# Both directions of a gated linear recurrence in one product per level, worked head by head

## What is computed

```python
def hgrn2_bidir(q, v, k_f, k_b, lf_f, lf_b, s0_f, s0_b):
    o_f = gla_chunk_scan(q, k_f, v, lf_f, s0_f)
    o_b = flip(gla_chunk_scan(flip(q), flip(k_b), flip(v), flip(lf_b), s0_b))
    return o_f + o_b
```

## Time and profile before

| what | us |
|---|---|
| median of three runs | 2602.84 |
| the profiled execution | 2599.3 |
| its span on the core | 2597.6 |
| PE busy in the span | 2484.4 |
| DVE busy | 1622.0 |
| ACT busy | 886.6 |
| the stage of the recurrence | 1287.3 to 1764.3 |

### The profile page before, as it was taken

The page is one execution under the profiler, slowest core; times in us unless marked ns, Lnnn a source line. Parts: engine busy times, 40 slices in busy tenths (PEclk is TensorE's granted clock), DMA queues, the critical chain, the costliest instruction groups (busy, mean ns, idle before and its releaser), DMA issues. The chain is left out here.

```text
span 2597.6 us, 39539 instructions
## 1 busy us (share of the span) xinstructions
PE 2484.4 (96%) x16809; PEld 1336.3 (51%) x16809; DVE 1622.0 (62%) x2112; ACT 886.6 (34%) x1061; POOL 26.8 (1%) x60
## 2 busy tenths in 40 slices
PE   7999889999999999999999999979989999999997
PEld 4457664444444444444767776764434444444443
DVE  6688747544444443645477878786766777774243
ACT  5118316332233232323354544452332222222121
POOL 0010000010000000000000000000000000000000
PEclk9999999999999999999999999999999999999999
DMA  9127563111111124343210000021101211113442
GB/s 328 31 73 235 192 212 131 33 49 49 48 48 48 48 77 111 106 120 130 56 31 18 25 26 25 18 97 50 33 17 52 61 49 48 48 55 106 112 112 87
DMA packets 302918, 207.37 MB, mean 80 GB/s; under 512 B 11296, under 2 KB 298174, under 8 KB 302143
## 3 DMA queue, kind: packets, MB, share of 16 engines
q1 hardware_dynamic: 301910, 205.08, 26.3%
q10 hardware_dynamic: 873, 0.32, 0.1%
HBM read 191.22 MB, written 13.64 MB: 79 GB/s over the span
## 5 line engine op out<-in xcount | busy, mean ns | idle before, releaser
L200 PE MATMUL ps<-hT,arena 128*128 128x512 bf16 (+1 forms) x6240 | 1337.3, 376 | 13.3 <-DVE hT L705 4.9
L200 PEld LDWEIGHTS ps<-hT,arena 128*128 128x128 bf16 x6240 | 609.1, 98 | 739.0 <-issue 17.1
L1917 PE MATMUL ps<-arena 128*128 128x512 bf16 x2112 | 458.7, 379 | 3.0 <-DVE arena L1899 3.0
L1917 PEld LDWEIGHTS ps<-arena 128*128 128x128 bf16 x2112 | 206.3, 98 | 252.2 <-DVE arena L1899 5.3
L2170 DVE SCALAR_TENSOR_TENSOR arena<-ps,vec,arena 128x945 f32<-128x945 f32 (+2 forms) x176 | 215.1, 1222 | 70.1 <-ACT arena L2156 50.7
L2137 DVE SCALAR_TENSOR_TENSOR arena<-ps,vec,arena 128x1023 f32<-128x1023 f32 (+1 forms) x88 | 106.8, 1276 | 177.8 <-ACT arena L2127 177.8
L1899 DVE TENSOR_TENSOR arena<-hT,arena 128x2816 bf16<-128x2816 f32 (+2 forms) x44 | 93.7, 2157 | 164.8 <-ACT arena L1893 164.6
L1893 ACT ACTIVATE arena<-hT 128x2816 bf16<-128x2816 f32 (+2 forms) x44 | 77.8, 1798 | 240.1 <-DMA hT<-w_down_dram 112.6
L2988 PE MATMUL ps<-arena 128*128 128x128 f32 (+1 forms) x896 | 103.2, 272 | 21.6 <-DVE arena L3309 21.6
L2084 DVE TENSOR_TENSOR arena<-hT,arena 128x2048 bf16<-128x2048 f32 x44 | 100.9, 2292 | 28.1 <-ACT arena L2051 27.8
L2988 PEld LDWEIGHTS ps<-arena 128*128 128x128 f32 (+1 forms) x896 | 98.5, 187 | 25.6 <-DVE arena L3309 24.0
(11 more groups left out here) (421 smaller groups left out, 2468.9 us busy)
## 6 DMA issues: line engine op xcount, KB each, us to landing
xT<-ada_w_dram SPq DMA_DIRECT2D x24, 1024.0 KB, 5.9
hT<-w_up_dram SPq DMA_DIRECT2D x44, 512.0 KB, 5.0
hT<-ffn_up_dram SPq DMA_DIRECT2D x44, 512.0 KB, 5.0
hT<-w_down_dram SPq DMA_DIRECT2D x30, 704.0 KB, 7.1
hT<-ffn_down_dram SPq DMA_DIRECT2D x30, 704.0 KB, 6.9
arena<-w_in_dram SPq DMA_DIRECT2D x33, 512.0 KB, 3.9
xT<-w_mod_dram SPq DMA_DIRECT2D x16, 1024.0 KB, 6.1
arena<-w_mod_dram SPq DMA_DIRECT2D x8, 1024.0 KB, 19.2
```

Of the source, the lines that this page charges most:

```text
L200: last = pe.matmul(out, lhs(a, kt), rhs(b, kt, i), start=start and kt == 0 and (a, b) == (0, 0), stop=stop and kt == n_k - 1 and (a, b) == ...
L1917: last = pe.matmul(self.bank(u), self.part(u, a, kt), self.g[:, b, kt, cols], start=kt == 0 and (a, b) == (0, 0), stop=kt == FT - 1 and (a ...
```

## The change

The two directions of a head are worked together. At a level, the keys of the forward direction stand in the left halves and its queries in the right ones, and for the backward direction the other way round. So one tile (`keys_side`) takes both directions' keys, 1024 columns full, and another (`queries_side`) both directions' queries; one product of 8 full chunks gives the scores of both, and one masked copy of 1024 columns, with the masks of both directions in one, takes them over. The diagonal adds both directions in PSUM. The scores are multiplied by the values once per head. There are 28 levels in all in place of 56, each with two exponentials.

The tiles for this need room: keys and b of both directions are kept for two heads, those of even heads in the space of the residual stream, which is away in this stage; the state's first block and the chunk decays move into the freed half of the masks; `x` has four buffers, two per level, so `subtract` of a level waits for the product two levels before. The order of a head is written anew on all engines: the projections of the next head come as V0, V1, z forward, z backward, query, gate, and those of head 0 all stand ahead of its levels. The weight tiles are loaded in this order, and the extra gates' pieces are cut anew (8 in place of 9).

```diff
-                    quarter = k.masks[:, d, l, :].rearrange("p (b h r) -> p b h r", h=2, r=m)[:, :, 1 - d, :]
+                    quarter = k.masks[:, 0, l, :].rearrange("p (b h r) -> p b h r", h=2, r=m)[:, :, 1 - d, :]
...
-    keys, b = take(2, TT), take(2, TT)
-    x = take(3, T)
+    odd_keys, odd_b = take(2, TT), take(2, TT)
+    x = take(4, T)
...
-    state0 = take(P)
-    chunk_decay = take(NCH)
+    state0 = k.masks[:, 1, 0, :]
+    chunk_decay = k.masks[:, 1, 1, 0:NCH]
+    even_keys = [scratch_x(k)(d * TT, TT) for d in range(2)]
+    even_b = [scratch_x(k)(11 * T // 2 + d * TT, TT) for d in range(2)]
...
+            def diagonal(h):
+                pe.wait_ge(k_ready, unit(h, 1) + 1)
+                pe.wait_ge(q_scaled, h + 1)
+                def both(out, c):
+                    for d in range(2):
+                        last = pe.matmul(out, x_tokens(keys(h, d))[:, c * P:(c + 1) * P], q[:, h % 2, c * P:(c + 1) * P],
+                                         start=d == 0, stop=d == 1)
+                    return last
+                chunk_job((h, "diagonal"), range(T // P), both)
+            def level(h, l):
+                pe.wait_ge(x_ready, NL * h + l + 1)
+                still, moving = keys_side(h, l), queries_side(h, l)
+                chunk_job((h, "level", l), range(T // P), lambda out, c: pe.matmul(
+                    out, still[:, c * P:(c + 1) * P], moving[:, c * P:(c + 1) * P], start=True, stop=True))
...
+            for h in range(HG_HEADS):
+                turned_keys(h, 0)
+                if h:
+                    sum_of_squares(h - 1)
+                diagonal(h)
+                level(h, 0)
+                state_products(h, 0)
+                front(h + 1, V0)
+                front(h + 1, V1)
+                level(h, 1)
+                turned_keys(h, 1)
+                carried(h, 0)
+                fill(("mid", h))
+                level(h, 2)
+                state_products(h, 1)
+                front(h + 1, ZF0)
+                front(h + 1, ZF1)
+                level(h, 3)
+                carried(h, 1)
+                front(h + 1, ZB0)
+                front(h + 1, ZB1)
+                level(h, 4)
+                front(h + 1, QUERY)
+                level(h, 5)
+                level(h, 6)
+                fill(("end", h))
+                front(h + 1, GATE)
...
+                for i, side in enumerate((keys_side(h, l), queries_side(h, l))):
+                    act.wait_ge(sub_done, 2 * (NL * h + l) + i + 1)
+                    act.activation(side, side, ACT.Exp).then_inc(exp_done, 1)
...
+            for h in range(HG_HEADS):
+                if h:
                     squares(h - 1)
+                level(h, 0)
+                turned_keys(h, 0)
+                if h:
+                    inverse_root(h - 1)
+                level(h, 1)
+                decays(h, 1)
+                front(h + 1, V0)
+                front(h + 1, V1)
+                weights_hi(h + 1, V1)
+                turned_keys(h, 1)
+                level(h, 2)
+                query_decays(h, 1)
+                level(h, 3)
...
-                front(n + 1, Z0)
-                front(n + 1, Z1)
-                softplus_parts(n + 1)
-                weights_hi(n + 1, Z1)
-                level(n, 5)
-                level(n, 6)
-                front(n + 1, V0)
-                forget_parts(n + 1)
-                front(n + 1, GATE)
...
+                front(h + 1, ZF0)
+                front(h + 1, ZF1)
+                softplus_parts(h + 1, 0)
+                weights_hi(h + 1, ZF1)
+                level(h, 4)
+                forget_parts(h + 1, 0)
+                front(h + 1, ZB0)
+                front(h + 1, ZB1)
+                softplus_parts(h + 1, 1)
+                weights_hi(h + 1, ZB1)
+                level(h, 5)
+                front(h + 1, QUERY)
+                weights_hi(h + 1, QUERY)
+                forget_parts(h + 1, 1)
+                level(h, 6)
+                decays(h + 1, 0)
+                query_decays(h + 1, 0)
+                front(h + 1, GATE)
+                weights_hi(h + 1, GATE)
...
-                i = NL * n + l - 3
+                i = NL * h + l - 2
...
+                dve.tensor_tensor(left, mid_f, left_f, ALU.subtract)
+                dve.tensor_tensor(right, mid_b, right_b, ALU.subtract).then_inc(sub_done, 1)
+                left, right = halves_of(queries_side(h, l), m)
+                dve.tensor_tensor(left, left_b, mid_b, ALU.subtract)
+                dve.tensor_tensor(right, right_f, mid_f, ALU.subtract).then_inc(sub_done, 1)
...
+                dve.wait_ge(exp_done, 2 * (NL * h + l) + 1)
+                for d in range(2):
+                    side = halves_of(keys_side(h, l), LEVELS[l])[d]
+                    dve.tensor_tensor(side, side, halves_of(x_tokens(keys(h, d)), LEVELS[l])[d], ALU.mult)
+                dve.wait_ge(exp_done, 2 * (NL * h + l) + 2)
+                side = queries_side(h, l)
+                dve.tensor_tensor(side, side, q[:, h % 2, :], ALU.mult).then_inc(x_ready, 1)
...
+            def select(h, l):
+                job = (h, "level", l)
+                by_chunk = lambda v: v.rearrange("p (c r) -> p c r", r=P)
+                mask = mask_u[:, l, :].unsqueeze(1).to_broadcast((P, T // P, P))
                 wait_made(dve, job)
-                s_, use = slot((n, "level", NL if l == 0 else l - 1))
-                dve.wait_ge(read[s_], use + 1)
-                dve.copy_predicated(queries(att), mask, queries(banks(job))).then_inc(read[slot(job)[0]], 1)
+                wait_read(dve, (h, "level", l - 1) if l else (h, "diagonal"))
+                dve.copy_predicated(by_chunk(att), mask, by_chunk(banks(job))).then_inc(read[slot(job)[0]], 1)
...
+                chain_states(h, 0)
+                weigh(h, 1)
+                decayed_keys(h, 1)
+                decayed_queries(h, 0)
+                weights_lo(h + 1, V1)
+                subtract(h, 2)
+                if h:
                     finish(h - 1)
...
-                subtract(n, 5)
-                select(n, 3)
-                subtract(n, 6)
-                softplus(n + 1)
-                weights_lo(n + 1, Z1)
-                weigh(n, 5)
-                weigh(n, 6)
-                select(n, 4)
-                forget(n + 1)
...
+                select(h, 1)
+                weigh(h, 2)
+                subtract(h, 3)
+                take_fill(("mid", h))
+                select(h, 2)
+                weigh(h, 3)
+                chain_states(h, 1)
+                decayed_queries(h, 1)
+                subtract(h, 4)
+                select(h, 3)
+                weights_lo(h + 1, ZF1)
+                softplus(h + 1, 0)
+                weigh(h, 4)
+                subtract(h, 5)
+                forget(h + 1, 0)
+                select(h, 4)
+                weigh(h, 5)
+                subtract(h, 6)
+                softplus(h + 1, 1)
+                weights_lo(h + 1, ZB1)
+                select(h, 5)
+                weigh(h, 6)
+                weights_lo(h + 1, QUERY)
+                forget(h + 1, 1)
+                key_distance(h + 1, 0)
+                select(h, 6)
+                wait_read(dve, (h, "level", 6))
...
+                decayed_keys(h + 1, 0)
+                subtract(h + 1, 0)
+                if h < LAST_HEAD:
+                    take_fill(("end", h))
+                scale_q(h + 1)
+                subtract(h + 1, 1)
```

More of the change, by code:

```diff
@@ L2908, in wait_made, with wait_read @@
         eng.wait_ge(made[s], use + 1)
+    def wait_read(eng, job):
+        s, use = slot(job)
+        eng.wait_ge(read[s], use + 1)
     def x_tokens(t):
@@ L2938, in _ @@
                 stream.load(sp, n)
-            s, use = slot((last_unit, "front", GATE))
-            sp.wait_ge(made[s], use + 1)
+            wait_made(sp, (LAST_HEAD, "front", GATE))
+            sp.wait_ge(o_made, LAST_HEAD)
             out.load(sp, 0)
@@ L2950, in _, with front @@
         def _(pe):
-            def front(n, piece):
-                if not has(n, piece):
+            def front(h, piece):
+                if h > LAST_HEAD:
                     return
-                job, tile = (n, "front", piece), tile_of(n, piece)
+                job, tile = (h, "front", piece), tile_of(h, piece)
                 stream.ready(pe, tile)
@@ L2976, in chunk_job @@
                 last.then_inc(made[slot(job)[0]], 1)
-            def level(n, l):
-                pe.wait_ge(x_ready, NL * n + l + 1)
-                v = x[:, buffer(n, l), :]
-                d, m = units[n][1], LEVELS[l]
-                whole = 2 * m < P
-                rows = slice(0, P) if whole else slice(d * m, (d + 1) * m)
-                columns = slice(0, P) if whole else slice((1 - d) * m, (2 - d) * m)
-                def product(out, c):
-                    chunk = v[:, c * P:(c + 1) * P]
```

(11 more changed lines are left out.)

470 lines of the change are left out of this document (199 added, 271 removed).

## The result

Four runs of the changed kernel gave 2629.46 to 2632.91 us, median **2630.8**; four of the kernel before 2598.31 to 2603.51, median 2601.0. The ratio is **1.0116** [1.0098, 1.0133]: slower by 29.8 us. The forecast was 2627, range 2607 to 2648. The profiled execution has a span of 2628.7 us (2597.6 before), a mean granted clock of 0.974.

What follows compares the result with a forecast made beforehand. TensorE (PE), busy 96% of the span, was taken as the bound. Less work (-51), more waits (+72) and the clock (+4) gave +25 us on 2599.3; the median lay 3.5 higher, so about 2627, range 2607 to 2648.

Steps and rivals of the forecast that it cites:

- PE loses 51.0 us: PE in the changed stage: fewer level products save 43.8 us, fewer products of scores by values 7.2.
- DVE and ACT stay as loaded: DVE and ACT, per head: about 0.2 us saved in weighing, still 56 exponentials, while PE gets lighter.
- The selection at 1.3: DVE's masked copy of 1024 contiguous columns: 1.3 us each, bounds 1.3 and 2.6.
- slower yet: Rival: DVE's selection takes 2.6 us, with the clock bound +10, giving about 2655 us; chance 0.08.
- Level 6 is where it breaks: Before level 6, heads 0 to 2: a 28 us ACT and DVE chain makes PE wait 16, 16, about 10; together 42.
- the sum: Whole execution: -51 for PE's work, +72 for waits, +4 for the clock, giving +25 us.
- The other waits: PE elsewhere: start 6.8 us, head changes 21.5, last head 26, tail 2; all waits about 100 for 28.2.
- The clock: +4, bounds 0 to 14: PE products after four long waits run at half clock, adding 4 us, bounds 0 and 14.
- the 5 to 8: Last head: if each short burst of PE started cold, the sum would be some 5 to 8 us higher.
- Nothing outside the stage changes: Outside the changed stage: the mask takes as many operations and the next stage starts from the same barrier.
- The rival "faster", 2582: Levels weighed in time ahead of level 6: 42 of waits and 4 for the clock go, -21 us; chance 0.09.

Runs made afterwards that it cites:

- x1: Changed kernel with, on ACT alone, the weight split that waits for its load moved behind the forget gate and level 6's exponentials: 2618.4 us, ratio 1.0065.
- x2: Changed kernel with, on ACT alone, level 6's exponentials moved right behind those of level 5: 2611.0 us, ratio 1.0041.
- x6: Changed kernel reordered: ACT's split and level 6 exponentials earlier; DVE's low part, level 6 weighing and finish earlier; PE's gate projection between levels 5 and 6: 2582.6 us.
- x7: Changed kernel with PE making unread identity products during its long waits ahead of level 6 and of last-head levels 1, 4, 5, 6: 2617.8 us, ratio 1.0066.
- x4: Changed kernel with, on DVE alone, the last head's finish moved ahead of the values tile's low part and level 2's subtraction: 2623.3 us, ratio 1.0088.
- x3: Changed kernel with, on PE alone, an extra-gates piece and the next gate's projection put between levels 5 and 6: 2615.0 us, ratio 1.0050.
- x5: Changed kernel with ACT's level 6 exponentials right behind level 5's, and DVE selecting 5 and weighing 6 before softplus and low part: 2614.8 us, ratio 1.0054.

## Why the prediction came out as it did

- **"PE loses 51.0 us."** The count holds (448 records of L3015 for 28 products). PE's busy time fell by 32.7 only, because 45.3 us of its work in the stage ran at half clock (3.4 before). Half the difference, 21 us, is our estimate of what that puts on it; with it PE's work at full clock fell by some 54.
- **"DVE and ACT stay as loaded."** ACT does (234 us in the stage and 232). DVE has 19.5 us less, 377.7 and 358.2, and 13.4 of that are the selections (49.9 for L3326, 36.5 for L3372). PE's waits grew all the same.
- **The selection at 1.3.** Measured 1.304; the upper bound of 2.6, and with it "slower yet", was wrong. (The parts of that rival, 9 + 12 + 10 on 2627, make 2658 and not 2655.)
- **"Level 6 is where it breaks": waits of 16, 16, 10.** Measured 15.4, 15.5, 9.5; the chain was 27.5 us for 28. x1 confirms low part, load and split as 6 us of it, x2 the place of the exponentials, and x6 that the moves together remove it. This step carried the sign: without its 40.3 us the sum for the stage (+25.6) is below zero.
- **The other waits.** Start 5.4 us for 6.8; head changes 6.1, 6.1 and 3.2 for 7.8, 7.8 and 6 (the smaller slot waits did not come in the first two); last head 22.4 for 26; tail 1.7 for 2.0. With level 6 and what is too small to list the waits are 86.8 for "about 100".
- **"The clock: +4, bounds 0 to 14."** This term was mis-sized: some 21 us more busy time at half clock (the estimate above), where the upper bound was 14. The forecast priced slow products after the four longest waits. The trace has half clock also after the 3.67 us waits of the head changes, and in nearly the whole last head; x7 gives back 8.3 us in the stage, 13.0 by the medians, and it still has five short stretches at half clock. How much of the 21 us the whole time bears is not shown beyond these 8.3. The Trainium skill, "TensorE: Matmul & The Clock Gate", section "HAM oscillation", which the prediction set beside its sum, describes bursts between waits for DMA that each start cold. The last head shows it after waits for DVE (3.5 to 3.8 us for 1.95), and the 5.1 us that x7 saves there lie at the lower end of the 5 to 8 that the prediction gave for it.
- **Why the sum still holds.** Stage: -51 + 58.3 of waits + 18.3 = +25.6 (forecast -51 + 72 + 4 = +25). The 18.3 are no reading of their own: they are what is left when 51 is set against the 32.7 that PE's busy time fell by. The clock's 21 above and a fall of 54 give the same sum. The errors in waits and clock belong together in part: a product that runs longer ahead of a DVE operation shortens the wait behind it and shows as busy time. The forecast had the waits at full clock, the profile shows them partly as slow products. The agreement of the sums to 1 us is in part luck.
- **The 4 us beyond it** are outside the stage. "Nothing outside the stage changes" holds for the operations; the edits outside it change the places of tiles and the order of two weight tiles. The medians less the stages are 2123.8 before and 2128.0 after, and 2123.2 to 2126.8 in the experiments. In the profiled executions the stage begins 2.5 us later than before (at 1289.95 for 1287.45), and 835.9 us follow it for 832.9, so the difference lies on both sides. What makes it was not settled.
- **The rival "faster", 2582**, said what would decide: "if levels were weighed in time". x6 does that, and has 2582.6. Its mechanism was right, and its condition was not met by this order. That the numbers agree to 1 us is luck in part: x6 has 49.8 us of waits in the stage where the rival's sum leaves some 58, still has 24.7 us of PE's work at half clock where that sum has no cost for the clock, and contains the move of x4, which the rival does not have.

## What to carry to other kernels

Work taken from the bounding engine is worth only as much as its neighbours' lead allows: before such a change, walk the chain of the tightest hand-over through every queue (here DVE, SP, DMA, ACT, DVE, PE) and compare it with the work the bounding engine still has in that time. An operation that waits for a load belongs behind all that the bounding engine waits for (x1), or the load must be issued early enough (x6); here one such wait on ACT delayed everything behind it in ACT's order. After moving one link, look where the next wait ends: x3 and x5 moved the wait to the score product, and of the kernels tried only x6, with all moves together, removed the level 6 waits without a new long one.

## What the runs showed of the hardware

- Half clock came after waits shorter than expected. A product after 1.98 us of waiting took 3.68 us, with waits of 6.58, 1.13 and 0.59 us in the 24 us ahead of it; in the kernel before, one after 2.08 us ran at full speed. The length of the last wait alone does not tell: in x7 the product of level 6 ran slow after a wait of 3.08 us with 13.6 us of products ahead of it.
- A slow clock costs time also on an engine with waits, where its operation stands in a ring with another engine's: 5.94 us a level at full clock, 7.2 to 7.5 at half.
- A masked copy of 1024 contiguous columns takes 1.30 us in the mean of the 28 of the changed kernel. In the kernel before, 512 columns in runs of one or two columns take 1.29 to 1.32, and 512 in longer runs 0.69 to 0.75, over all 56.
